# DeltaNet merge levels on packed 32x32 blocks, one tile of tokens per step

## What is computed

```python
a_mat = eye + jnp.where(strict, jnp.einsum("bhid,bhjd->bhij", ki, ki) * decay * bi[..., :, None], 0.0)
rhs = jnp.concatenate([vi * bi[..., None], ki * (bi * jnp.exp(gcum))[..., None]], axis=-1)
sol = lax.linalg.triangular_solve(a_mat, rhs, left_side=True, lower=True, unit_diagonal=True)
u, w = sol[..., :dv], sol[..., dv:]
v_new = u - jnp.einsum("bhik,bhkv->bhiv", w, state)
```

## Time and profile before

| | us |
|---|---|
| median of 3 runs | 1045.88 (1045.09 to 1047.46) |
| the profiled execution, whole | 1045.29 |
| its span | 1043.5 |
| TensorE busy | 1010.7 (97%) |
| VectorE, ScalarE, GpSimd busy | 612.4, 510.9, 122.4 |
| merge levels, first y to the last update | 785.06 to 806.8 |

### The profile page before, as it was taken

One profiled execution on the slowest core, in us unless ns is written; L12 is line 12 of the kernel. 1 busy time (PEld: TensorE's weight loads), 2 busy tenths in 40 slices (PEclk: granted clock), 3 DMA queues, 4 the chain that ended last, 5 costly groups with the idle time before them and its releaser, 6 DMA issues.

```text
span 1043.5 us, 14457 instructions
## 1 busy us (share of the span) xinstructions
PE 1010.7 (97%) x5188; PEld 837.0 (80%) x5188; DVE 612.4 (59%) x749; ACT 510.9 (49%) x718; POOL 122.4 (12%) x232
## 2 busy tenths in 40 slices
PE   7999999998999999999999999999997999999997
PEld 5888888777878888887888888778886878888886
DVE  5645444668575445457545445768895575545544
ACT  6444343556364434446444443677765264444342
POOL 4700000051000000001000000115541310000000
PEclk9999999999999999999999999999998999999999
DMA  9655655461256555554765555363323036565541
GB/s 321 232 192 172 199 183 188 152 221 42 81 175 209 180 188 195 193 169 144 234 204 164 201 177 184 105 239 132 133 102 122 1 121 228 175 201 167 195 161 40
DMA packets 123816, 175.43 MB, mean 168 GB/s; under 512 B 7233, under 2 KB 98562, under 8 KB 123778
## 3 DMA queue, kind: packets, MB, share of 16 engines
q1 hardware_dynamic: 121824, 171.00, 48.9%
q0 software_dynamic: 864, 3.15, 0.8%
q10 hardware_dynamic: 1090, 0.77, 0.3%
HBM read 173.85 MB, written 1.05 MB: 168 GB/s over the span
## 4 chain that ended last, share of the span: by engine, by line
PE 87%; DVE 8%; ACT 4%; issue 1%; DMA 0%; POOL 0%; ACTq 0%; DVEq 0%; POOLq 0%
PE banks L1058 18%; PE banks L1060 17%; PE banks L1059 17%; PE banks L1096 9%; PE banks L1098 9%; PE banks L1103 9%; PE banks L1132 2%; DVE xT_low L1651 1%; PE banks L1362 1%; DVE w_low L1632 1%; DVE mixer_arena L1881 1%; ACT xT_high L697 1%; PE banks L1076 1%; ACT mixer_arena L924 0%; DVE diag_inverse L1937 0%
## 5 line engine op out<-in xcount | busy, mean ns | idle before, releaser
L1632 DVE TENSOR_TENSOR w_low<-w_raw,w_high 128x2048 fp32r<-128x2048 f32 x153 | 351.9, 2303 | 214.0 <-ACT w_high L675 186.9
L1058 PE MATMUL banks<-w_high,xT_high 128*128 128x512 f32 (+1 forms) x880 | 350.5, 398 | 7.8 <-DVE xT_low L1651 7.2
L1060 PE MATMUL banks<-w_high,xT_low 128*128 128x512 f32 (+1 forms) x880 | 343.4, 390 | 0.0
L1059 PE MATMUL banks<-w_low,xT_high 128*128 128x512 f32 (+1 forms) x880 | 342.5, 389 | 0.0
L675 ACT ACTIVATE w_high<-w_raw 128x2048 fp32r<-128x2048 f32 x108 | 206.4, 1911 | 113.8 <-PE banks L1103 113.8
L1058 PEld LDWEIGHTS banks<-w_high,xT_high 128*128 128x128 f32 x880 | 166.2, 189 | 44.0 <-DVE xT_low L1651 8.5
L1060 PEld LDWEIGHTS banks<-w_high,xT_low 128*128 128x128 f32 x880 | 166.0, 189 | 35.3
L1059 PEld LDWEIGHTS banks<-w_low,xT_high 128*128 128x128 f32 x880 | 166.5, 189 | 31.9
L1096 PE MATMUL banks<-w_high,hT_high 128*128 128x512 f32 x320 | 125.0, 391 | 0.0
L1098 PE MATMUL banks<-w_low,hT_high 128*128 128x512 f32 x320 | 124.7, 390 | 0.0
L661 ACT ACTIVATE w_high<-w_raw 128x2048 fp32r<-128x2048 f32 x47 | 89.7, 1918 | 22.3 <-PE banks L1060 19.2
(11 more groups left out here) (253 smaller groups left out, 878.4 us busy)
## 6 DMA issues: line engine op xcount, KB each, us to landing
w_raw<-in_l_ffn_w_in SPq DMA_DIRECT2D x172, 512.0 KB, 4.6
w_raw<-in_l_ffn_w_out SPq DMA_DIRECT2D x88, 512.0 KB, 3.9
w_raw<-in_b_w_in SPq DMA_DIRECT2D x32, 512.0 KB, 4.4
w_raw<-in_a_w_in SPq DMA_DIRECT2D x10, 512.0 KB, 4.2
w_raw<-in_a_w_out SPq DMA_DIRECT2D x8, 512.0 KB, 4.6
w_raw<-in_b_w_out SPq DMA_DIRECT2D x8, 512.0 KB, 3.8
gain_rows<-in_l_norms POOLq DMA_DIRECT2D x6, 512.0 KB, 4.1
w_raw<-in_l_ffn_w_in SPq DMA_DIRECT2D x8, 256.0 KB, 4.4
```

The lines of the kernel that those rows point to most:

```text
L1058: pe.matmul(dst, sh, wh, start=start, stop=False)
L1059: pe.matmul(dst, sh, wl, start=False, stop=False)
L1060: return pe.matmul(dst, sl, wh, start=False, stop=stop)
L1632: dve.tensor_tensor(wlo[:, c % 3, :], raw[:, c % 3, :], whi[:, c % 3, :], ALU.subtract).then_inc(w_lo, 1)
```

## The change

The levels are reordered and their data is kept packed for longer.

- A step now covers one tile of tokens t, eight matrices, in place of one block b, four matrices. There are two steps per level.
- Level one works on the packed W and T (`Wp`, `Tp`, 32x32 blocks in four strips). y is 64 matmuls of 32x32 (`y16`), the products are 128: for T and, in the same manner, for W. VectorE subtracts both (128x256 each). The transposes of Tm and ScalarE's copies of them are gone.
- POOL masks N in place, on the diagonal 32x32 blocks only, four instructions of 32x16x32.
- `spread` makes T ahead of W. The unpacking stands behind the first level: POOL copies T (and W of t = 1), ScalarE W of t = 0.
- `y16` stands between the two halves of unit 16 on TensorE, `turn_back(6)` and `kq(1)`, `kq(2)` have moved ahead into unit 15, `kq(3)` lies behind the first products.
- Level two updates T's quarter for strip 1 only (three matmuls per matrix in place of four); level three is as before, 512 columns at once.
- On ScalarE `hi` of unit 19 has moved behind the levels, `v_rows(6)` ahead. On VectorE `lo` of unit 17 is split into two halves, one ahead of the levels and one within them, and `lo` of units 18 and 19 now stands in the recurrence, behind the vn0 products and ahead of o0.

The diff, cut to its core:

```diff
+        Wp = diag[:, 1, :].rearrange("p (m c) -> p m c", m=2 * GH)
+        Tp = diag[:, 2, :].rearrange("p (m c) -> p m c", m=2 * GH)
@@ POOL
-                for q in range(4 * len(LEVELS)):
-                    masked(q)
+                pool.wait_ge(packed, 4)
+                for at in STRIPS:
+                    v = Nm[at].rearrange("p b (i c) -> p (b i) c", i=HG)[:, :, at]
+                    pool.tensor_tensor(v, v, lvl[at, at].unsqueeze(1).to_broadcast([32, 2 * GH, 32]), ALU.mult
+                                       ).then_inc(n16_ready, 1)
+                for t in range(TT):
+                    pool.wait_ge(t_done, t + 1)
+                    for at in STRIPS[0:2]:
+                        last = pool.tensor_copy(of_tile(Tm[at, :, at], t), of_tile(Tp[at], t))
+                    last.then_inc(t_spread, 1)
+                for pair in (STRIPS[2:4], STRIPS[0:2]):
+                    for at in pair:
+                        last = pool.tensor_copy(of_tile(Wm[at, :, at], 1), of_tile(Wp[at], 1))
+                    last.then_inc(w_spread[1], 1)
@@ ACT
                     if s == 16:
+                        y_copy(0)
+                        z_of(c, 1)
+                        break
+                    hi(base + s + 3, s + 3)
+                    if s == 15:
                         v_rows(6)
...
-                    if s == 15:
-                        unpack()
...
+                act.wait_ge(t_done, 1)
+                act.wait_ge(wt0_zero, 2)
+                for at in STRIPS[2:4]:
+                    last = act.activation(of_tile(Wm[at, :, at], 0), of_tile(Wp[at], 0), ACT.Copy)
+                last.then_inc(w_spread[0], 1)
+                y_copy(1)
+                for t in range(TT):
+                    act.wait_ge(prod_ps, 2 + t + 1)
+                    for up_, down_ in PAIRS:
+                        last = act.activation(of_tile(Wm[up_, :, down_], t), by_matrix4(PS[up_, t, 0:256]),
+                                              ACT.Copy, scale=-1.0)
+                    last.then_inc(w32_done, 1)
+                y_copy(2)
...
+                hi(base + 19, 19)
@@ PE
+                    if s == 15:
+                        turn_back(6)
                     if s == 16:
-                        turn_back(6)
+                        y16()
...
+                for t in range(TT):
+                    pe.wait_ge(y_cp, t + 1)
+                    pe.wait_ge(unpacked, 2)
+                    pe.wait_ge(p_done, 3)
+                    for j, b, i in matrices(t):
+                        for at in STRIPS:
+                            y = Dm[at, t, 32 * j:32 * j + 32]
+                            pe.matmul(PS[at, 6 + t, 32 * j:32 * j + 32], Wp[at, 4 * b + i, :], y,
+                                      start=True, stop=True)
+                            last = pe.matmul(PS[at, 6 + t, 256 + 32 * j:288 + 32 * j], y, Wp[at, 4 * b + i, :],
+                                             start=True, stop=True)
+                    last.then_inc(prod_ps, 1)
+                kq(3)
@@ DVE
+                for t in range(TT):
+                    dve.wait_ge(prod_ps, t + 1)
+                    for k, m in enumerate((Tp, Wp)):
+                        v = of_tile(m, t)
+                        last = dve.tensor_tensor(v, v, by_matrix4(PS[:, 6 + t, 256 * k:256 * k + 256]), ALU.subtract)
+                    last.then_inc(t_done, 1)
...
+                p_of(3)
+                lo_half(base + 17, 17, 1)
...
                 for hg in range(NG):
                     new_values(0, hg, 0, Dm[:, hg, :], "vn0p", "vn0")
+                lo(base + 18, 18)
+                lo(base + 19, 19)
```

More of the change, by code:

```diff
@@ L68 @@
 CT = 3 * GH
-LEVELS = (16,)
-NLEV = 3
 B = 16
@@ L73 @@
 TOP, LOW = slice(0, 64), slice(64, 128)
-PAIRS = ((slice(0, 32), slice(32, 64)), (slice(64, 96), slice(96, 128)))
+STRIPS = [slice(32 * q, 32 * q + 32) for q in range(4)]
+PAIRS = ((STRIPS[0], STRIPS[1]), (STRIPS[2], STRIPS[3]))
 STAGES = ["ffn", "swa", "ffn", "ffn", "gdn", "ffn"]
@@ new lines, in gdn @@
+                kq(3)
+                for t in range(TT):
+                    pe.wait_ge(t_done, t + 1)
+                    for j, b, i in matrices(t):
+                        for up_, down_ in PAIRS:
+                            last = pe.matmul(PS[down_, 4 + t, 32 * j:32 * j + 32],
+                                             heads(Nm[:, b, :])[up_, i, down_], Tp[up_, 4 * b + i, :],
+                                             start=True, stop=True)
+                    last.then_inc(y_ps, 1)
@@ L1990, in gdn @@
                     if s == 15:
[L1991 to L1992 removed]
+                        for b in range(3):
+                            p_of(b)
                     if s == 16:
[L1994 removed]
+                        lo_half(base + 17, 17, 0)
                     if s <= 8:
```

254 lines of the change are left out of this document (89 added, 165 removed).

## The result

The changed kernel takes 1043.72 us (median of 12 runs, 1041.28 to 1045.91) against 1045.63 for the kernel before (12 runs beside them, 1045.00 to 1049.48); the ratio is 0.997, with a 95% interval of 0.9961 to 0.998. So it is faster by 0.3%, some 3 us by the ratio, where 1046.7 was forecast. The profiled execution took 1043.71 us for a span of 1042.0, 1.5 less than before. The busy line of the page (columns as in the earlier trace rows) and the line of TensorE's instruction queue, 26 packets where the kernel before had 24. Over the whole run that is more than 128 records a packet: in both kernels four stretches of some 600 to 670 records each, outside the DeltaNet, show no packet, and why is open. From 717.86 to 853.66 us, around the levels, ten packets stand against 1246 records, 125 for each.

The account below looks back on a forecast made before the run. TensorE bounds the kernel, its dense levels limited by instruction packets 5.8 us apart. Later vn0p +0.35, shorter half clock behind it -0.2, moved splits +0.7 sum to +0.85 on 1045.88: 1046.7 us, range 1036 to 1050.

Parts of the forecast that it names:

- What bounds the levels: In the merge levels TensorE's dense narrow matmuls are limited by instruction packets, four in series, 23.2 us.
- edge 428: Packet boundary in the first products, at their 228th record; TensorE arrives at 788.8 and stops 4.8 us.
- 5.8 us a packet, asked for 168 records ahead: In the levels, each packet follows the last by 5.8 us when TensorE runs dry, requested about 168 records early; chance 0.42.
- rival B: In the levels a packet needs 4.2 us, requested 128 records ahead; 4 to 8 us gained, 1040; chance 0.17.
- Three stops: TensorE stops at packet edges 300, 428 and 556, in the first products and products32; gaps of 1 to 5 us.
- The clock: TensorE's clock falls to half by about 793 until vn0p has run some 3 us; vn0p at 807.2, 805.8 at full.
- The tail: From vn0p to out_proj: 17.89 us before, -0.2 for less half clock, +0.7 for splits of units 18 and 19.
- The sum: Whole kernel: +0.35 - 0.2 + 0.7 = +0.85 us, giving 1046.7.
- Rival A: In the levels instructions come in time; 12.8 us gained, 1033, or 1037 with a clock drop; chance 0.22.
- Rival C: In the levels a packet needs 6.8 us; vn0p at 810.4, +4.0 us, 1049.9; chance 0.15.
- Rival D: Narrow matmuls in y16 and products start slowly, 23 ns each, where fewer tiles take turns; 1047.8; chance 0.04.
- the rule weighed: Skill's 25 ns start-to-start floor would make y16 and first products take 9.6 us instead of 3.1; judged contradicted by trace.

Follow-up runs that it names:

- e9: The changed kernel with the first y behind the second half of unit 16 instead of ahead of it; 1043.91 us.
- b1: The kernel before with only the change's order of the weight splits, levels left unpacked; 1044.77 us, ratio 0.9984 to the kernel before.
- e5: The changed kernel with the first level's W made from the new T by VectorE's block transposes, 128 matmul records fewer; 1032.78 and 1033.23 us.
- e11: The kernel of e5 plus one extra 128x256 fp32 matmul (0.43 us) ahead of products32; 1032.84 us, ratio 0.9868 to the kernel before.
- e7: The changed kernel with VectorE's splits of units 17 and 18 right at unit 16; slower than without, vn0p 0.9 us later.
- e8: The changed kernel with both the block transposes of e5 and the early splits of e7; 6 us above e5.
- e12: e11 with VectorE's split of unit 17's second half behind the transposes and of unit 18 ahead of products64; 3 us above e11.
- e3: The changed kernel with kq(3) issued between the two tiles' first products instead of behind both; 1043.49 us, ratio 0.9957 to the kernel before.
- e6: The changed kernel with kq(3) between the tiles and four extra 128x512 fp32 matmuls, results unused, where stops would be; ratio 0.9935 to the kernel before.

## Why the prediction was wrong, point by point

- **What bounds the levels.** Right: TensorE's instruction packets, 128 records each. The forecast edge 428, the 228th record of the first products, is where the stop stands (225 records of the products in the trace before it), and e9 has 128 between two stops.
- **The step that failed: 5.8 us a packet, asked for 168 records ahead.** From a packet that TensorE waited for to the next it measured 3.5 to 4.1 us in every kernel with packed levels and no weights in flight (3.83 from stop to stop in e9), and the packet of 785.16 begins about 1.0 us after TensorE passes the edge before, 128 records ahead. That is rival B's mechanism and nearly its 4.2 us. The 168 was misread for one of its two packets besides: at 788.05 us in the kernel before TensorE had 112 records behind it, 187 short of the edge at 299. The 3.45 us between resuming and the next packet, which I took from the earlier trace rows as a property of the fetch, is 1.1 in the changed kernel and 1.0 to 1.7 in its variants without weights in flight. I had one instance and gave it 0.42. So 5.8 was a true reading of the kernel before and no constant. Why before and b1 wait 3.5 and 4.6 us there is open; in before it wasn't the weights, since the earlier trace rows show none. Those levels go group by group with waits between, but no run tells whether that is the reason.
- **Its consequence.** Three stops were forecast at 300, 428 and 556; there was one, of 2.2 us. From kq(0) vn0p was to come at 40.4 us (807.2 - 766.82) and came at 36.2. This one term is -3.8 instead of +0.35. Rival B had 33.2 to 35.7 by the clock, and the measured value lies just beyond its end at half clock: from the stop on TensorE was the limit itself.
- **The clock.** Right that it falls and stays until behind vn0p; it fell at the stop, some 3 us sooner against kq(0) than forecast, and lasted 17.1 us. The levels behind it were indeed no longer supply-bound. That this was the dearest part, by my estimate 6 us, the prediction does not say: it priced the clock as 1.4 us at vn0p.
- **The tail.** The sum is right, -0.2 + 0.7 on 17.89 makes 18.4 and 18.45 was measured, in part by luck: half clock reached 3.9 us into it, not 3.1. VectorE's timeline has o0 right behind the two splits, as forecast, in place of the idle 3.39 us of the earlier trace rows; the queue is full from vn0 to R1:

```profile
809.15 4.48 DVE L1632 TENSOR_TENSOR w_low<-w_raw,w_high 128x2048 fp32r<-128x2048 f32 x2
813.55 1.28 DVE L2056 TENSOR_TENSOR mixer_arena<-banks,mixer_arena 128x512 f32<-128x512 f32 x2
814.75 0.68 DVE L2061 TENSOR_TENSOR mixer_arena<-banks,gdn_small 128x512 f32<-128x512 f32 x1
```

- **The sum.** Forecast +0.85; the stretch shows -3.26. The median moved by -1.9 us, between the likeliest case and rival B's 1040; inside the range of 1036 to 1050, which was that wide for the rivals' sake, outside the 1044 to 1048 of the forecast alone, and on the other side of no change.
- **Rival A** would have had 1033 to 1037. The kernels that remove the stop, e5 and e11, are just below: 1032.8. Its sum fits, but a kernel with 128 records fewer.
- **Rival C** named the cause for other kernels: with weights in flight a packet came 1.5 to 1.9 us later (e7, e8, e12). In the changed kernel, as it said against itself, none are.
- **Rival D and the rule weighed.** Start to start was 8.8 ns in y16 (128 records in 1.12 us), 9.8 with two in a row on a strip, 19 with four: all below the 25 ns that the Trainium skill, "TensorE: Matmul & The Clock Gate", section "Wait — 56ns, not 53.3ns?", states, so here the measurement decides.

## What to carry to other kernels

Count instructions as a resource: a dense run of matmuls so narrow that 128 records take less than 4 us can run ahead of its packets, and a record saved (here 128 of them by four block transposes on an idle VectorE) is worth far more than its own 10 ns. A stop of TensorE can cost more than its length, by the half-rate work behind it, so look for dense work that can stand where it would stop. And an early step on an engine that has time frees a buffer, which starts a load, which can hold up the instructions.

## What was not expected of the hardware

- With a stop of 2 us came 17 us of half clock, through all of the narrow work and 3.9 us of the 128x128 matmuls behind it, though TensorE was busy for 16.64 of 17.00 us of it.
- 3.5 us of extra matmuls cost nothing: with the same order and no fill the ratio is 0.9957 (e3), with the fill 0.9935 (e6), 3.3 us less in the traces' stretch, though the intervals of the ratios overlap.
- With weight loads in flight (264 GB/s on average from 784 to 789 us in e7) a 16 KB packet of instructions began up to 1.9 us later: it was not served ahead of them.
- The narrow matmuls' pace depends on how often the strip changes: 9, 10 and 19 ns a record for one, two and four in a row.
